# One of the weight sums of a gate/up pair: from VectorE into an adding DMA on GpSimd's queue

## The reference

```
h = rmsnorm(x, g_pre_ffn[l])
g, u = jnp.split(h @ w_gate_up[l], 2, axis=-1)
x = x + rmsnorm((jax.nn.silu(g) * u) @ w_down[l], g_post_ffn[l])
```

## Time and profile before

| | |
|---|---|
| time, median of 3 runs | 764.51 us (764.49 to 765.46) |
| profiled execution, its own time | 764.42 us |
| its span, first to last instruction | 762.5 us |
| mean granted clock of TensorE | 0.999 |
| PE busy | 756.0 us (99% of the span) |
| DVE, ACT, POOL busy | 523.3, 400.7, 332.8 us |
| the stage of the 18 pairs | 455.8 to 637.2 us |

### The profile page before, as it was taken

One profiled execution on the slowest core, in us unless ns is written; L12 is line 12 of the kernel. 1 busy time (PEld: TensorE's weight loads), 2 busy tenths in 40 slices (PEclk: granted clock), 3 DMA queues, 4 the chain that ended last, 5 costly groups with the idle time before them and its releaser, 6 DMA issues.

```text
span 762.5 us, 12110 instructions
## 1 busy us (share of the span) xinstructions
PE 756.0 (99%) x4314; PEld 666.0 (87%) x4314; DVE 523.3 (69%) x725; ACT 400.7 (53%) x668; POOL 332.8 (44%) x219
## 2 busy tenths in 40 slices
PE   9999999999999999999999999999999999999997
PEld 7788888888888888888889989999999999888885
DVE  4979989987566665289327667888777773444474
ACT  5763287776686776632255444555555552323243
POOL 6937365957678688234563420000000003444462
PEclk9999999999999999999999999999999999999999
DMA  9653542232222422225561124333333313313312
GB/s 337 180 162 89 159 114 68 57 88 78 63 63 70 117 63 63 83 77 192 161 199 56 57 80 118 92 98 109 110 110 110 110 63 130 100 66 109 110 55 110
DMA packets 102732, 81.54 MB, mean 107 GB/s; under 512 B 3488, under 2 KB 91560, under 8 KB 102696
## 3 DMA queue, kind: packets, MB, share of 16 engines
q1 hardware_dynamic: 102504, 81.06, 34.4%
q10 hardware_dynamic: 192, 0.01, 0.0%
HBM read 76.85 MB, written 3.68 MB: 106 GB/s over the span
## 4 chain that ended last, share of the span: by engine, by line
PE 98%; issue 1%; POOL 0%; DVE 0%; ACT 0%; POOLq 0%; DVEq 0%
PE ps L582 26%; PE ps L561 12%; PE ps L563 12%; PE ps L562 12%; PE ps L887 8%; PE ps L886 8%; PE ps L885 8%; PE ps L648 3%; PE ps L806 3%; PE ps L795 2%; PE ps L778 1%; PE ps L780 1%; PE ps L701 1%; PE ps L700 1%; PE ps L642 0%
## 5 line engine op out<-in xcount | busy, mean ns | idle before, releaser
L1419 POOL TENSOR_TENSOR wn_lo<-raw,wn_hi 128x1024 fp32r<-128x1024 f32 x18 | 43.1, 2396 | 236.6 <-ACT wn_hi L968 236.6
L561 PE MATMUL ps<-h_hi,w_hi 128*128 128x512 f32 (+1 forms) x320 | 123.6, 386 | 0.0
L563 PE MATMUL ps<-h_hi,w_lo 128*128 128x512 f32 (+1 forms) x320 | 121.8, 381 | 0.0
L562 PE MATMUL ps<-h_lo,w_hi 128*128 128x512 f32 (+1 forms) x320 | 121.6, 380 | 0.0
L1535 POOL TENSOR_TENSOR w_lo<-raw,w_hi 128x1024 fp32r<-128x1024 f32 x30 | 78.3, 2615 | 30.5 <-ACT w_hi L1116 30.1
L1937 DVE TENSOR_TENSOR d_lo<-act,d_hi 128x512 fp32r<-128x512 f32 x18 | 41.8, 2328 | 56.0 <-ACT d_hi L1363 56.0
L1419 POOL TENSOR_TENSOR w_lo<-raw,w_hi 128x1024 fp32r<-128x1024 f32 x20 | 48.7, 2441 | 58.2 <-ACT w_hi L968 53.1
L563 PEld LDWEIGHTS ps<-h_hi,w_lo 128*128 128x128 f32 x320 | 60.2, 188 | 11.5
L562 PEld LDWEIGHTS ps<-h_lo,w_hi 128*128 128x128 f32 x320 | 60.4, 189 | 9.8
L561 PEld LDWEIGHTS ps<-h_hi,w_hi 128*128 128x128 f32 x320 | 60.3, 188 | 9.8
L885 PE MATMUL ps<-t_hi,sum_hi 128*128 128x256 f32 x216 | 61.1, 283 | 0.0
(11 more groups left out here) (283 smaller groups left out, 2172.7 us busy)
## 6 DMA issues: line engine op xcount, KB each, us to landing
raw<-in_w_in SPq DMA_DIRECT2D x40, 512.0 KB, 4.5
raw<-in_w_gate_up SPq DMA_DIRECT2D x26, 512.0 KB, 3.8
raw<-in_w_down SPq DMA_DIRECT2D x22, 512.0 KB, 4.1
raw<-in_w_gate_up SPq DMA_DIRECT2D x36, 256.0 KB, 4.2
raw<-in_w_out SPq DMA_DIRECT2D x8, 512.0 KB, 4.4
x_t<-in_first SPq DMA_DIRECT2D x8, 256.0 KB, 6.7
wq_raw<-in_first SPq DMA_DIRECT2D x8, 256.0 KB, 6.2
x_in<-in_x SPq DMA_DIRECT2D x4, 512.0 KB, 7.1
```

The costliest lines, as they stand in the source:

```text
L561: mm(acc, whi_c, a_hi_, start=first, stop=False)
L562: mm(acc, whi_c, a_lo_, start=False, stop=False)
L563: return mm(acc, wlo_c, a_hi_, start=False, stop=last)
L1419: nc.gpsimd.tensor_tensor(lo[:, at(u), :], raw[:, at((d % 2) * 2 + u), :], hi[:, at(u), :], sub).then_inc(w_lo_done, 1)
```

## The change

The last of the four quarters is no longer read as it is. When the three loads of a pair have landed, POOL issues a DMA from SBUF to SBUF with an adding write: q3 <- q3 + q2, inside the slot. The slot's last quarter then holds the first sum s0 (before: an instruction of DVE, into its own buffer). The DMA counts on a new semaphore, `pair_summed`, 16 a pair. POOL issues the one of pair p when pair p has been loaded and the DMA of pair p - 1 has landed; in POOL's program the loop of 18 stands after the last w_lo split of the plain tiles and before the wn_lo splits.

With that:
- The four quarters of the slot (2 x 1024 columns) are the four operands "quart", split in two instructions of 1024 columns each on ACT and on DVE; the second waits for `pair_summed` (ACT) or for ACT's. The "sums" are three: s1 = q3' + q0, then s1 - q2 (= q3 + q0) and s1 + q1. They are split in one instruction of 1536 columns each on ACT and DVE. DVE's first instruction of a pair now waits for `pair_summed`.
- ACT's order in a window: the two quarter roundings, `first_kept`, `fifth_kept`, the sums' rounding, `sixth_kept`, silu. Before, a sums' rounding stood between `first_kept` and `fifth_kept` and the other after `sixth_kept`.
- PE's products keep their order and sizes. The second one reads the fourth quarter; the wait for the third set of operands moves ahead of the third product.
- The buffers quart and sum change sizes (4Q and 3Q) and places; SP's `raw_free` waits for 3 sums a pair instead of 4.

```diff
@@ -246,20 +246,20 @@
-    quart_hi, quart_lo = [sb("quart_hi0", 3 * Q, F32R)], [sb("quart_lo0", 3 * Q, F32R)]
-    sum_hi, sum_lo = [sb("sum_hi0", 4 * Q, F32R)], [sb("sum_lo0", 4 * Q, F32R)]
+    quart_hi, quart_lo = [sb("quart_hi0", 4 * Q, F32R)], [sb("quart_lo0", 4 * Q, F32R)]
+    sum_hi, sum_lo = [sb("sum_hi0", 3 * Q, F32R)], [sb("sum_lo0", 3 * Q, F32R)]
-    quart_hi.append(sb("quart_hi1", 3 * Q, F32R))
-    quart_lo.append(sb("quart_lo1", 3 * Q, F32R))
+    sum_hi.append(sb("sum_hi1", 3 * Q, F32R))
+    sum_lo.append(sb("sum_lo1", 3 * Q, F32R))
-    sum_hi.append(sb("sum_hi1", 4 * Q, F32R))
-    sum_lo.append(sb("sum_lo1", 4 * Q, F32R))
+    quart_hi.append(sb("quart_hi1", 4 * Q, F32R))
+    quart_lo.append(sb("quart_lo1", 4 * Q, F32R))
     sums = []
-        sums.append(sb(f"sums{n}", 4 * Q))
+        sums.append(sb(f"sums{n}", 3 * Q))
...
@@ -906,15 +906,15 @@
             pe.wait_ge(parts_hi_done, p * 3 + 2)
             pe.wait_ge(parts_lo_done, p * 3 + 2)
             pe.wait_ge(summed_up, p * 2 + 2)
-            product(c, s_hi_, s_lo_, 0, *t_sum(0), True).then_inc(product_done, 1)
-            pe.wait_ge(product_kept, p * 3 + 1)
-            product(m, s_hi_, s_lo_, Q, *t_sum(2), False).then_inc(product_done, 1)
-            product(gate, q_hi_, q_lo_, Q, *h_quarter(1, 0), False).then_inc(product_done, 1)
+            product(c, q_hi_, q_lo_, 3 * Q, *t_sum(0), True).then_inc(product_done, 1)
             pe.wait_ge(parts_hi_done, p * 3 + 3)
             pe.wait_ge(parts_lo_done, p * 3 + 3)
+            pe.wait_ge(product_kept, p * 3 + 1)
+            product(m, s_hi_, s_lo_, 0, *t_sum(2), False).then_inc(product_done, 1)
+            product(gate, q_hi_, q_lo_, Q, *h_quarter(1, 0), False).then_inc(product_done, 1)
             pe.wait_ge(product_kept, p * 3 + 3)
-            product(m, s_hi_, s_lo_, 2 * Q, *t_sum(1), False).then_inc(product_done, 1)
-            product(c, s_hi_, s_lo_, 3 * Q, *h_quarter(1, 1), False).then_inc(product_done, 1)
+            product(m, s_hi_, s_lo_, Q, *t_sum(1), False).then_inc(product_done, 1)
+            product(c, s_hi_, s_lo_, 2 * Q, *h_quarter(1, 1), False).then_inc(product_done, 1)
             pe.wait_ge(summed_up, p * 2 + 5)
             product(m, q_hi_, q_lo_, 2 * Q, *t_sum(3), False).then_inc(product_done, 1)
 
...
@@ -1296,22 +1296,21 @@
         def quarters_hi(p, v):
 
             sc.wait_ge(up_in, p * 48 + 48)
-            run(quart_hi[v][:, 0:2 * Q], raw[:, 2 * v, :], ACT.Copy)
-            run(quart_hi[v][:, 2 * Q:3 * Q], raw[:, 2 * v + 1, 0:Q], ACT.Copy).then_inc(parts_hi_done, 1)
-
-        def sums_hi(p, v, n):
-
-            sc.wait_ge(sum_made, p * 4 + (n + 3))
-            part = slice(2 * Q * n, 2 * Q * (n + 1))
-            run(sum_hi[v][:, part], sums[v][:, part], ACT.Copy).then_inc(parts_hi_done, 1)
+            run(quart_hi[v][:, 0:2 * Q], raw[:, 2 * v, :], ACT.Copy).then_inc(parts_hi_done, 1)
+            sc.wait_ge(pair_summed, p * 16 + 16)
+            run(quart_hi[v][:, 2 * Q:4 * Q], raw[:, 2 * v + 1, :], ACT.Copy).then_inc(parts_hi_done, 1)
+
+        def sums_hi(p, v):
+
+            sc.wait_ge(sum_made, p * 3 + 3)
+            run(sum_hi[v][:, :], sums[v][:, :], ACT.Copy).then_inc(parts_hi_done, 1)
 
...
@@ -1345,10 +1344,9 @@
 
             quarters_hi(p + 1, 1 - v)
             first_kept(p, v)
-            sums_hi(p + 1, 1 - v, 0)
             fifth_kept(p, v)
+            sums_hi(p + 1, 1 - v)
             sixth_kept(p, v)
-            sums_hi(p + 1, 1 - v, 1)
             silu_gates(p, v)
 
         sc.wait_ge(tile_done, T_DOWN)
...
@@ -1591,6 +1589,12 @@
             for u in range(2):
                 split(d, u)
 
+        for p in range(SEVENS):
+            gp.wait_ge(up_in, p * 48 + 48)
+            if p:
+                gp.wait_ge(pair_summed, p * 16)
+            pair_ = raw[:, 2 * (p % 2) + 1, :]
+            gp.dma_start(pair_[:, Q:2 * Q], pair_[:, 0:Q], accum_op=ALU.add).then_inc(pair_summed, 16)
         with gp.Fori(T_DOWN // 2, (T_END - LAST) // 2) as d:
             for u in range(2):
                 split(d, u, wn_hi, wn_lo)
...
@@ -1969,39 +1973,28 @@
 
             return raw[:, 2 * v + n // 2, n % 2 * Q:(n % 2 + 1) * Q]
 
-        def sum_of(p, v, i, x_, y_, made=None):
-
-            if made:
-                ve.wait_ge(sum_made, p * 4 + made)
-            tt(sums[v][:, i * Q:(i + 1) * Q], x_, y_, ALU.add).then_inc(sum_made, 1)
-
         def sum_part(v, i):
             return sums[v][:, i * Q:(i + 1) * Q]
 
-        def first_sums(p, v):
-
-            ve.wait_ge(up_in, p * 48 + 48)
-            sum_of(p, v, 0, quarter(v, 3), quarter(v, 2))
-            sum_of(p, v, 2, quarter(v, 0), quarter(v, 3))
-
-        def second_sum(p, v):
-            sum_of(p, v, 1, sum_part(v, 0), quarter(v, 0), 1)
-
-        def third_sum(p, v):
-            sum_of(p, v, 3, sum_part(v, 1), quarter(v, 1), 3)
-
-        def quarters_rest(p, v):
-
-            ve.wait_ge(parts_hi_done, p * 3 + 1)
-            both = raw[:, 2 * v:2 * v + 2, :].rearrange("p u n -> p (u n)")
-            tt(quart_lo[v][:, :], both[:, 0:3 * Q], quart_hi[v][:, :], sub).then_inc(parts_lo_done, 1)
-
-        def sums_rest(p, v, n):
-
-            ve.wait_ge(sum_made, p * 4 + 4)
-            ve.wait_ge(parts_hi_done, p * 3 + (n + 2))
+        def three_sums(p, v):
+
+            ve.wait_ge(pair_summed, p * 16 + 16)
+            tt(sum_part(v, 0), quarter(v, 3), quarter(v, 0), ALU.add).then_inc(sum_made, 1)
+            ve.wait_ge(sum_made, p * 3 + 1)
+            tt(sum_part(v, 1), sum_part(v, 0), quarter(v, 2), sub).then_inc(sum_made, 1)
+            tt(sum_part(v, 2), sum_part(v, 0), quarter(v, 1), ALU.add).then_inc(sum_made, 1)
+
+        def quarters_rest(p, v, n):
+
+            ve.wait_ge(parts_hi_done, p * 3 + (n + 1))
             part = slice(2 * Q * n, 2 * Q * (n + 1))
-            tt(sum_lo[v][:, part], sums[v][:, part], sum_hi[v][:, part], sub).then_inc(parts_lo_done, 1)
+            tt(quart_lo[v][:, part], raw[:, 2 * v + n, :], quart_hi[v][:, part], sub).then_inc(parts_lo_done, 1)
+
+        def sums_rest(p, v):
+
+            ve.wait_ge(sum_made, p * 3 + 3)
+            ve.wait_ge(parts_hi_done, p * 3 + 3)
+            tt(sum_lo[v][:, :], sums[v][:, :], sum_hi[v][:, :], sub).then_inc(parts_lo_done, 1)
 
         def up_2(p, v):
 
...
@@ -2026,24 +2019,20 @@
             stt(act[:, at(p + PLAIN), 0:HALF], bank(4 - 4 * v, HALF), -1.0, silu[:, 0, 0:HALF],
                 ALU.mult, ALU.mult).then_inc(act_done, 1)
 
-        first_sums(0, 0)
-        second_sum(0, 0)
-        third_sum(0, 0)
-        quarters_rest(0, 0)
-        sums_rest(0, 0, 0)
-        sums_rest(0, 0, 1)
+        three_sums(0, 0)
+        quarters_rest(0, 0, 0)
+        quarters_rest(0, 0, 1)
+        sums_rest(0, 0)
         up(1)
         ve.sem_inc(summed_up, 4)
 
         def window(p, v):
 
             n, w = p + 1, 1 - v
-            first_sums(n, w)
-            second_sum(n, w)
-            third_sum(n, w)
-            quarters_rest(n, w)
-            sums_rest(n, w, 0)
-            sums_rest(n, w, 1)
+            three_sums(n, w)
+            quarters_rest(n, w, 0)
+            quarters_rest(n, w, 1)
+            sums_rest(n, w)
             up_2(p, v)
             gate_two(p, v)
 
```

More of the change, by code:

```diff
@@ L248, in build @@
     top[0] = sets_at
-    quart_hi, quart_lo = [sb("quart_hi0", 3 * Q, F32R)], [sb("quart_lo0", 3 * Q, F32R)]
-    sum_hi, sum_lo = [sb("sum_hi0", 4 * Q, F32R)], [sb("sum_lo0", 4 * Q, F32R)]
+    quart_hi, quart_lo = [sb("quart_hi0", 4 * Q, F32R)], [sb("quart_lo0", 4 * Q, F32R)]
+    sum_hi, sum_lo = [sb("sum_hi0", 3 * Q, F32R)], [sb("sum_lo0", 3 * Q, F32R)]
     assert top[0] <= rows_at
     top[0] = rows_at
-    quart_hi.append(sb("quart_hi1", 3 * Q, F32R))
-    quart_lo.append(sb("quart_lo1", 3 * Q, F32R))
+    sum_hi.append(sb("sum_hi1", 3 * Q, F32R))
+    sum_lo.append(sb("sum_lo1", 3 * Q, F32R))
     assert top[0] <= zone2 - 4 * HALF
     top[0] = w_hi_at
-    sum_hi.append(sb("sum_hi1", 4 * Q, F32R))
-    sum_lo.append(sb("sum_lo1", 4 * Q, F32R))
+    quart_hi.append(sb("quart_hi1", 4 * Q, F32R))
+    quart_lo.append(sb("quart_lo1", 4 * Q, F32R))
     sums = []
     for n in range(2):
-        top[0] = w_hi_at + 4 * 4 * Q if n else rows_at - 4 * 4 * Q
-        sums.append(sb(f"sums{n}", 4 * Q))
+        top[0] = (rows_at if n else rows_at - 4 * 3 * Q) + 4 * 3 * Q * n
+        sums.append(sb(f"sums{n}", 3 * Q))
     top[0] = sets_at
@@ L357, in build @@
     early_made, t_hi_done, t_done = sems("early_made", "t_hi_done", "t_done")
-    up_in, sum_made, parts_hi_done, parts_lo_done = sems(
-        "up_in", "sum_made", "parts_hi_done", "parts_lo_done")
+    up_in, sum_made, parts_hi_done, parts_lo_done, pair_summed = sems(
+        "up_in", "sum_made", "parts_hi_done", "parts_lo_done", "pair_summed")
     product_done, product_kept, summed_up = sems("product_done", "product_kept", "summed_up")
@@ L512, in raw_free @@
         def raw_free(n):
```

(5 more changed lines are left out.)

## The result

The changed kernel takes 771.83 us (median of 3 runs, 771.30 to 771.88), against 764.51 us: a ratio of 1.0090, 95% interval 1.0067 to 1.0112. It is slower, as forecast (768.5 us, range 766.0 to 773.5), and 3.3 us further than forecast. The profiled execution took 771.88 us with a span of 770.1 us (762.5 before), at a mean granted clock of 0.995 (0.999).

What follows compares the result with a forecast made beforehand. TensorE was taken to bound the kernel, holding 98% of the chain of waits. 764.42 us profiled + 4.1 start stall + 0 for DVE and ACT off the path = 768.5 us, range 766.0 to 773.5.

Steps and rivals of the forecast that it cites:

- a stall at the start at full clock: Before pair 0's first product: PE waits 4.1 us behind pair 0's adding DMA, clock full; chance 0.52.
- Steady state hidden: Steady pairs: an adding DMA of up to 8.3 us between the loads' landing and DVE's first reading costs nothing.
- The step's rule for what lies beyond it: Steady pairs: each us of adding DMA above 8.3 us costs up to 17 us.
- ACT's copy, 0.17 us of slack: Each pair on ACT: the first product's copy leaves 0.17 us before PE's third product; cost taken as nothing.
- Rival 3: Each pair: ACT's first-product copy comes late for PE, up to 1.7 us in all, 770.2 us; chance 0.12.
- The chain from t0 to PE: Start of stage: from t0, the landing of pair 0's adding DMA, through DVE's act product to PE's start, 6.60 us.
- The price of the DMA: Pair 0's adding DMA: 4.7 us, landing at 453.3 us; bounds of the landing 450.9 and 455.2.
- rival 1: At the start stall: PE's clock falls, matmuls behind it run at half pace, up to 2.0 us, 770.5; chance 0.26.
- These two are covered: Pairs 1 and 2: their adding DMAs land before they are needed, pair 1's before 458.5 us.
- Rivals 2: Each pair: the adding DMA takes more than 8.3 us and bounds the pair; 803 for 10 us; chance 0.04.
- 4: PE's first product: finds its operands, pair 0's DMA landing below 449.2 us; time stays at 764.5; chance 0.05.
- rival 5: PE's pitch in the stage: shortened by fewer DVE reads, 762.9 us with no start stall; chance 0.01.

Runs made afterwards that it cites:

- experiment 2: Changed kernel with the first act product of up(1) put ahead of pair 0's sums on DVE: 768.11 us, ratio 1.0065.
- Experiment 6: Changed kernel with the first sums of pairs 0 and 1 made by DVE, 16 adding DMAs left: 764.48 us, ratio 1.0002.
- experiment 7: Kernel with pairs 0 and 1 on DVE, plus one or two spare 256 KB DMAs ahead of each adding DMA: 766.53 and 797.19 us.
- experiment 8: Changed kernel without DMAs, all 18 first sums on DVE: 765.90 us; then ACT's first-product copy also moved between the two roundings: 764.16 us.
- experiment 4: Changed kernel with SP's loads of pair 1 held back until pair 0's adding DMA has landed: 770.16 us, ratio 1.0072.
- 10: Changed kernel, pair 0's DMA ahead of POOL's last two splits, SP's loads from pair 2 on waiting for the previous pair's DMA: 765.25 us.
- Experiment 3: Changed kernel with 23 more matmuls keeping PE busy between the last plain tile and the first product: 769.77 us, ratio 1.0073.
- experiment 1: Changed kernel with pair 0's first sum made by DVE in the slot, the 17 other pairs keeping the adding DMA: 770.25 us, ratio 1.0078.
- 5: Changed kernel with all 18 adding DMAs, pair 0's issued ahead of POOL's last two splits: 769.67 us, ratio 1.0070.

## Why the prediction was right, and what it mis-sized

The direction and the range held. The case called most likely, a stall at the start at full clock (0.52), is not what happened; the stall with the clock's fall (0.26) is. The range took it in. Of the prediction's own signs of being wrong one came (a granted clock below 1.00 behind the gap), and a second seemed to (a releaser other than DVE), which experiment 2 settles for DVE.

- **Steady state hidden: right.** Experiment 6 is the proof (ratio 1.0002), experiment 7 the margin: some 5.9 us are hidden and some 10.1 are not, around the forecast's 8.3. In experiment 6 a slot is loaded at 488.33 and first read by DVE at 496.75, 8.4 us later. The step's rule for what lies beyond it was wrong in form: the loop runs over two slots.
- **ACT's copy, 0.17 us of slack: right.** 0.17 us in the trace after. Rival 3 did not come true here, and does as soon as the second rounding is 0.2 us later (experiment 8: 1.5 us of time, 1.75 of the stage, against 1.7 as worked out, though in unequal parts from pair to pair).
- **The chain from t0 to PE: right.** 6.70 us against 6.60, with DVE's act product as its end.
- **The price of the DMA: the first mis-sized term.** 4.7 us were taken for pair 0's and 6.1 measured, so the stall was 5.6 and not 4.1 us, inside the bounds of 1.7 to 6.0. The upper bound's 455.2 was near, but not its picture: the DMA did not wait for pair 1's loads, it landed at 454.44 and they at 456.11. Alone the DMA takes 3.2 to 3.3 us (experiments 4 and 10). The estimate by the Trainium skill ("DMA: Bandwidth & Descriptors", Anatomy of one DMA — SWDGE (gpsimd) path), 2.0 us plus the bytes over 436 GB/s, was 2.6 us; the plain copy's 2.2 us is near that, the adding one's 3.2 is not, and 6.1 beside loads is far from it.
- **The clock: rival 1 came true on top of the forecast.** 2.25 us lost against at most 2.0 as worked out, since the stall was longer. It was given a chance of 0.26 because a stall of 4.1 us was just as long as the 3.8 us after which the tail's rows show the fall. The stall of 5.6 us lasted well past that. Experiment 3 takes the fall away: 2.1 us. The argument against it, that a stall of 3 us would be over in time, does not hold in general: in experiments 4 and 7 the clock fell 2.2 and 2.3 us after the last matmul. The two terms are the 3.3 us between 768.5 and 771.83: PE started at 461.14 instead of 455.81, 5.33 - 4.1 = 1.2 us, and the clock 2.25, less 0.2 us that lie around the span and between profiled execution and median.
- **"These two are covered": true only behind the stall.** Pair 1's DMA landed at 460.07, not before 458.5, and DVE came to it at 461.51. Pair 2 was in time. But the cover was the stall itself: with pair 0 on DVE (experiment 1) or issued early (5), pair 1's DMA costs a gap of 3.8 us and the clock's fall. A reader who took from the prediction that pair 0 is the cause would have mended it and gained 1.6 to 2.2 us of 7.3.
- Rivals 2, 4 and 5 did not come true. For rival 5, a shorter pitch with less of DVE's reading, experiment 6 says no: ratio 1.0002, and a stage of 181.58 us against 181.4.

The cause, as the runs leave it: each adding DMA needs 3.2 us between the landing of a pair's loads and their first use. From pair 2 on that room is there. Pairs 0 and 1 do not have it, pair 0 because POOL's order puts its DMA behind the last split, pair 1 because its slot only comes free 7 us before it is needed. Beside pair 0's DMA, and beside pair 1's once pair 0 no longer stalls, the loads of the next pair are issued in the same moment, and the DMA takes 6.1 to 6.6 us instead.

Left open: why the loads and the DMA slow each other to this degree. The loads of pair 1 were slower too: DMA traffic goes on until about 455.1 us, where it ended at 453.6 before, though together they are only a quarter more bytes. Open too is why pair 1's DMA took 3.9 us in the changed kernel (3.8 and 3.7 in experiments 2 and 3), with no loads issued beside it.

## What to carry to other kernels

When work goes from an engine to a DMA, look at the first two uses by themselves: here a ring of two buffers that hides the DMA in the steady state hid it in neither of the first two, and the lateness of the second was invisible as long as the first stalled. Read beside each DMA what is issued in the same microsecond, and let the DMA on the path go first and the load with slack wait; here one such wait was worth 4.4 us. Where the load has no slack either, as pair 1's in experiment 4, the loss only moves. A stall of PE is to be priced with the clock behind it, which here added 2.25 us to 5.6. And a loss in each pair that no list of waits shows is found by comparing the length of the stage (experiment 8).
